# Layer normalization of a two-layer recurrent trunk: centering, root, folded parameters, and the order around the modulation chunks

## The reference

```python
mods = (silu(c) @ ada_w + ada_b).reshape(B, 3, 3, 1, D_MODEL)

def modulate(t, i):
    return t * (1.0 + mods[:, i, 1]) + mods[:, i, 0]

def residual(t, i, out, w):
    return _layer_norm(ALPHA * t + w * (1.0 + mods[:, i, 2]) * out, ln_g[i], ln_b[i])

x = residual(x, 0, _swiglu(modulate(x, 0), ...), 0.5)
# mixer: projection of modulate(x, 1), heads, output projection
x = residual(x, 1, mix, 1.0)
x = residual(x, 2, _swiglu(modulate(x, 2), ...), 0.5)
```

## Time and profile before

| | us |
|---|---|
| median of 3 runs | 2032.99 |
| lowest, highest | 2031.02, 2041.39 |
| the profiled execution's own time | 2035.65 |
| its span | 2033.8 |

### The profile page before, as it was taken

How to read it: one execution, slowest core, us unless ns; L and a number is a source line. 1 busy time by engine, 2 the same in 40 slices (tenths; PEclk the granted TensorE clock), 3 DMA queues, 4 the chain that set the end, 5 groups by cost and what they waited for, 6 DMA issues and landing times.

```text
span 2033.8 us, 33834 instructions
## 1 busy us (share of the span) xinstructions
PE 1812.7 (89%) x14564; PEld 1622.5 (80%) x14564; DVE 965.9 (47%) x1571; ACT 675.2 (33%) x927; POOL 223.5 (11%) x265
## 2 busy tenths in 40 slices
PE   6999998876899788999989999889759977799997
PEld 3899997775677567999979999788647756699996
DVE  2444445563333366454454444556443243665544
ACT  1332334352212235333353333444321122443333
POOL 1000012001000223000130001300010011410012
PEclk9999998888676678999999999998867665999999
DMA  8555545323232026444455554533322110434442
GB/s 302 187 206 188 176 149 190 98 89 130 94 95 68 18 76 212 144 147 153 148 176 197 179 200 148 177 132 104 109 73 95 49 36 32 142 114 154 148 146 78
DMA packets 85204, 272.37 MB, mean 134 GB/s; under 512 B 18976, under 2 KB 21312, under 8 KB 84800
## 3 DMA queue, kind: packets, MB, share of 16 engines
q1 hardware_dynamic: 85056, 270.22, 39.1%
HBM read 263.92 MB, written 6.26 MB: 133 GB/s over the span
## 4 chain that ended last, share of the span: by engine, by line
PE 77%; DVE 10%; ACT 5%; issue 3%; DMA 3%; POOL 2%; SPq 0%; DVEq 0%; ACTq 0%; POOLq 0%
PE psV L1767 10%; PE psV L1769 10%; PE psV L1768 10%; PE psA L1767 9%; PE psA L1768 8%; PE psA L1769 8%; DMA raw<-weights_dram 3%; PE psV L657 3%; PE psC L1782 2%; DVE wlo L2029 2%; PE psV L1793 2%; ACT whi L1928 1%; POOL ZT L2165 1%; PE psY L1782 1%; PE psA L1124 1%
## 5 line engine op out<-in xcount | busy, mean ns | idle before, releaser
L2029 DVE TENSOR_TENSOR wlo<-raw,whi 128x1024 fp32r<-128x1024 f32 x344 | 425.8, 1242 | 495.8 <-ACT whi L1928 493.8
L1928 ACT ACTIVATE whi<-raw 128x1024 fp32r<-128x1024 f32 x344 | 362.4, 1056 | 364.8 <-PE psV L1769 346.2
L1767 PE MATMUL psA<-XH,whi 128*128 128x320 f32 x1200 | 387.1, 323 | 50.6 <-DVE wlo L2029 34.4
L1768 PE MATMUL psA<-XL,whi 128*128 128x320 f32 x1200 | 379.9, 317 | 0.0
L1769 PE MATMUL psA<-XH,wlo 128*128 128x320 f32 x1200 | 379.4, 316 | 0.0
L1767 PEld LDWEIGHTS psA<-XH,whi 128*128 128x128 f32 x1200 | 234.4, 195 | 67.6 <-issue 62.7
L1767 PE MATMUL psV<-XH,whi 128*128 128x320 f32 x848 | 268.7, 317 | 13.2 <-DVE wlo L2029 7.2
L1769 PE MATMUL psV<-XH,wlo 128*128 128x320 f32 x848 | 264.9, 312 | 0.0
L1768 PE MATMUL psV<-XL,whi 128*128 128x320 f32 x848 | 264.9, 312 | 0.0
L1768 PEld LDWEIGHTS psA<-XL,whi 128*128 128x128 f32 x1200 | 234.5, 195 | 0.3
L1769 PEld LDWEIGHTS psA<-XH,wlo 128*128 128x128 f32 x1200 | 233.8, 195 | 0.0
(11 more groups left out here) (359 smaller groups left out, 2040.7 us busy)
## 6 DMA issues: line engine op xcount, KB each, us to landing
raw<-weights_dram SPq DMA_DIRECT2D x488, 512.0 KB, 3.4
ZS<-st_rw_dram SPq DMA_DIRECT2D x2, 768.0 KB, 4.5
S<-st_gla_dram SPq DMA_DIRECT2D x2, 768.0 KB, 4.4
o_glas_dram<-S SPq DMA_DIRECT2D x2, 768.0 KB
o_rws_dram<-ZS SPq DMA_DIRECT2D x2, 768.0 KB
CON<-consts_dram SPq DMA_DIRECT2D x1, 1288.5 KB, 10.2
XT<-xT_dram SPq DMA_DIRECT2D x1, 1280.0 KB, 9.8
yT_dram<-XT SPq DMA_DIRECT2D x8, 160.0 KB
```

The lines of the kernel that those rows point to most:

```text
L1767: mm(out, whi[:, n % SPL, k], hi[:, kt], start=first, stop=False)
L1768: mm(out, whi[:, n % SPL, k], lo[:, kt], start=False, stop=False)
L1928: activation(whi[:, n % SPL], raw[:, DENSE[n] % RAW], ACT.Copy).then_inc(hi_done, 1)
L2029: tt(wlo[:, n % SPL], raw[:, DENSE[n] % RAW], whi[:, n % SPL].bitcast(F32), ALU.subtract).then_inc(lo_done, 1)
```

## The change

- PLAN: "norm" comes directly after the product's step, ahead of all ada chunks.
- TensorE's `norm` opens both banks and multiplies ZSUM and QSUM before it waits for the last z and the last square.
- Centering: GpSimd's `center` is gone. VectorE subtracts the mean from ZT, tiles 0 and 1 ahead of the wait for the root, tile t + 2 behind the product of tile t.
- Root: ScalarE loads the table for Sqrt and takes the root; VectorE takes the reciprocal. ScalarE then loads the table for Silu where an FFN comes next.
- ln_g and ln_b of the norm before are folded into scale and shift of the modulation (in `unfold`), so that XM comes from ZT; XT is made by ScalarE one tile behind XM.
- Split of the next product's third chunk: ScalarE's part moves ahead of the last square, VectorE's part into `modulate`, at t == 3.
- GpSimd's sample modulation reads ZT and waits for `zn_ready`.

```diff
     def product(step, s, groups):
         chunks, left = two_groups(groups)
-        return [step] + chunks[:2] + [("norm", L, s)] + chunks[2:], left
+        return [step, ("norm", L, s)] + chunks, left
...
                 def norm(s):
-
-                    bank = bV.open()
                     pe.wait_ge(sem("zsum_ready"), s + 1)
-                    mm(bank[:, 0:TOK], con("mean1024", P), ZSUM[:], start=True, stop=False)
+                    means = []
+                    for x in (ZSUM, QSUM):
+                        bank = bV.open()
+                        mm(bank[:, 0:TOK], con("mean1024", P), x[:], start=True, stop=False)
+                        bV.close()
+                        means.append(bank)
                     pe.wait_ge(sem("z_ready"), (s + 1) * DT)
...
+                    def result(t):
+                        A.do(activation(XT[:, t], ZT[:, t], ACT.Identity, scale=lcol("ln_g", after, t),
+                                        bias=lcol("ln_b", after, t)), sem("x_ready"))
+
                     for t in range(DT):
                         if after is not None:
                             act.wait_ge(sem("zn_ready"), after * DT + t + 1)
...
+                        A.do(activation(XM[:, t, 0:SEQ], (XT if after is None else ZT)[:, t, 0:SEQ], ACT.Identity,
+                                        scale=scol(s, 1, t), bias=scol(s, 0, t)), sem("xm_prompt"))
+                        if after is not None and t:
+                            result(t - 1)
...
                 def product(n0, kts, s):
                     for d in range(DT):
-                        split_to(n0 + ((d + 1) * kts - 1) // 8 + 2)
+                        split_to(n0 + ((d + 1) * kts - 1) // 8 + (2 if d < DT - 1 else 3))
                         act.wait_ge(sem("z_ready"), s * DT + d + 1)
                         A.do(activation(SQ[:, d], ZT[:, d], ACT.Square), sem("sq_ready"))
 
-                    split_to(n0 + DT * kts // 8 + 2)
-
                 def norm(s):
+                    nc.scalar.preload_act_table(ACT.Sqrt)
                     act.wait_ge(sem("var_ready"), s + 1)
-                    rsqrt(A, VR[:], sem("sd_ready"))
+                    A.do(activation(VR[:], VR[:], ACT.Sqrt), sem("sd_ready"))
+                    if s % 3 != 0 and s < 3 * DEPTH - 1:
+                        nc.scalar.preload_act_table(ACT.Silu)
                     modulate(s + 1 if s < 3 * DEPTH - 1 else None, s)
...
                     if g == 3:
...
+                        s = 3 * L + i
+                        if s:
...
+                            V.settle()
+                            V.do(tt(rest, scale, affine("ln_b"), ALU.mult))
+                            V.settle()
+                            V.do(tt(shift, shift, rest, ALU.add))
+                            V.do(tt(scale, scale, affine("ln_g"), ALU.mult))
...
-                def modulate(s, after):
+                def modulate(s, after, n_next=0):
                     for t in range(DT + 2):
                         if t < DT and after is not None:
-
-                            vec.wait_ge(sem("zc_ready"), after * DT + t + 1)
                             V.do(tt(ZT[:, t], ZT[:, t], VR[:], ALU.mult), sem("zn_ready"))
+                            if t < DT - 2:
+                                V.do(tt(ZT[:, t + 2], ZT[:, t + 2], MN[:], ALU.subtract))
+                                V.settle()
+                        if t == 3:
+                            split_to(n_next + 2)
...
                     V.do(ts(VR[:], VR[:], 0.0, LN_EPS / ALPHA ** 2, ALU.max, ALU.add), sem("var_ready"))
-                    split_to(n_next + 2)
+                    for t in range(2):
+                        V.do(tt(ZT[:, t], ZT[:, t], MN[:], ALU.subtract))
                     vec.wait_ge(sem("sd_ready"), s + 1)
-                    modulate(s + 1 if s < 3 * DEPTH - 1 else None, s)
+                    V.do(nc.vector.reciprocal(VR[:], VR[:]))
+                    V.settle()
+                    modulate(s + 1 if s < 3 * DEPTH - 1 else None, s, n_next)
```

More of the change, by code:

```diff
@@ L1937, in modulate @@
                             act.wait_ge(sem("zn_ready"), after * DT + t + 1)
[L1938 to L1943, removed]
+                        if s is None:
+                            result(t)
+                            continue
+                        A.do(activation(XM[:, t, 0:SEQ], (XT if after is None else ZT)[:, t, 0:SEQ], ACT.Identity,
+                                        scale=scol(s, 1, t), bias=scol(s, 0, t)), sem("xm_prompt"))
+                        if after is not None and t:
+                            result(t - 1)
+                    if s is not None and after is not None:
+                        result(DT - 1)
                 def product(n0, kts, s):
                     for d in range(DT):
-                        split_to(n0 + ((d + 1) * kts - 1) // 8 + 2)
+                        split_to(n0 + ((d + 1) * kts - 1) // 8 + (2 if d < DT - 1 else 3))
                         act.wait_ge(sem("z_ready"), s * DT + d + 1)
                         A.do(activation(SQ[:, d], ZT[:, d], ACT.Square), sem("sq_ready"))
-                    split_to(n0 + DT * kts // 8 + 2)
                 def norm(s):
+                    nc.scalar.preload_act_table(ACT.Sqrt)
                     act.wait_ge(sem("var_ready"), s + 1)
-                    rsqrt(A, VR[:], sem("sd_ready"))
+                    A.do(activation(VR[:], VR[:], ACT.Sqrt), sem("sd_ready"))
+                    if s % 3 != 0 and s < 3 * DEPTH - 1:
+                        nc.scalar.preload_act_table(ACT.Silu)
                     modulate(s + 1 if s < 3 * DEPTH - 1 else None, s)
@@ L2043, in unfold, with affine @@
                         V.settle()
-                        V.do(ts(mods[:, i * 24 + 8:i * 24 + 16], mods[:, i * 24 + 8:i * 24 + 16], 1.0, None, ALU.add))
+                        shift, scale, rest = [mods[:, i * 24 + 8 * j:i * 24 + 8 * j + 8] for j in range(3)]
+                        V.do(ts(scale, scale, 1.0, None, ALU.add))
+                        s = 3 * L + i
+                        if s:
+                            def affine(name):
+                                k = PARC[name] + (s - 1) % 3 * DT
+                                return PAR[:, (s - 1) // 3, k:k + DT].unsqueeze(2).to_broadcast([P, DT, 9])
+                            V.settle()
[3 more added lines that the diff above has]
+                            V.do(tt(scale, scale, affine("ln_g"), ALU.mult))
                         V.mark(sem("mods_ready"))
@@ L2066, in product @@
                 def product(n0, kts, s, states=None):
+                    if s:
+                        vec.wait_ge(sem("x_ready"), s * DT)
                     for d in range(DT):
@@ L2157, in sums @@
                     G.mark(sem("zsum_ready"))
[L2159 to L2165, removed]
                 def modulate(s):
@@ L2170, in modulate @@
                     pool.wait_ge(sem("mods_ready"), s + 1)
[L2171 to L2173 removed]
                     for t in range(DT):
                         if s:
[L2176 to L2177 removed]
+                            pool.wait_ge(sem("zn_ready"), (s - 1) * DT + t + 1)
+                        G.do(tt(s8(mtmp[:, t % 2]), s8((ZT if s else XT)[:, t, SEQ:TOK]), by_sample(scol(s, 1, t, 1, DB)), ALU.mult))
                         G.settle()
```

13 lines of the change are left out of this document (4 added, 9 removed).

## The result

The changed kernel takes 2084.28 us in the median (2082.5 to 2086.92) against 2035.69 for the kernel before beside it (2031.02 to 2041.39): a ratio of 1.0238, 95% interval 1.0207 to 1.027. The forecast was 2070.5, with 2060 to 2082 as its range. The direction and the mechanism of the gaps hold; 2084.28 lies outside the range. The difference to the kernel before is 48.6 us, where the sum had 37.5: 11 us were missing from it. The other 2.7 of the 13.8 us are the kernel before, which had 2032.99 on record and has 2035.69 here.

What follows compares the result with a forecast made beforehand. The prediction took TensorE to bound the kernel, its gaps set by modulation chunk loads. 37.0 - 1.2 + 1.2 + 0.1 - 0.1 + 0.5 = 37.5 us on 2032.99 gave 2070.5, range 2060 to 2082.

Steps and rivals of the forecast that it cites:

- What bounds the gap: Behind the first four normalizations, modulation chunk loads queue behind VectorE's third-chunk split; 10.37 us from its end to the projection.
- D2's wlo: VectorE's split of the next product's third chunk, at the first normalization: ends at 320.6 instead of 311.36, +9.24 us.
- Rival A: Modulation chunk loads don't follow the third chunk's split; the arithmetic chain sets the start: 2030 us, not slower; chance 0.10.
- Copy 0.9 us after z, square 0.48, clamp 2.83 us after z: Start of the normalization: earlier mean copy gains 1.7 us, square without GpSimd's subtractions gains 0.7; clamp ends at 311.49.
- Reciprocal: In the normalization's root: VectorE's reciprocal of 128x320 takes 2.153 us; the root part loses 0.8 us.
- First XL: VectorE's first split activation after the normalization: x_split comes at 318.4, 2.8 us earlier than before.
- Next product: First projection matmul behind the first normalization moves from 321.73 to 331.0; the four gaps together cost 37.0 us.
- N4: Fifth normalization, no modulation chunks behind it: the next group starts at 1780.6 against 1780.47, +0.1 us.
- What comes back, and the clock at the gaps: Two first groups no longer paced by split activations, -1.2 us; lower granted clock after four longer gaps, +1.2 us.
- Rival B: GpSimd's sample modulation holds up VectorE's loop at four normalizations: 12.8 us more, so 2083; chance 0.10.
- Folding: Folding ln_g and ln_b: five times three VectorE operations on 72 elements; 0 to 5 us, 0.5 taken.
- case C: The five-chunk burst in the gaps takes 9.5 us instead of 10.37: 2067; included in the forecast's 0.80 chance.

Runs made afterwards that it cites:

- e1: The changed kernel with VectorE's split of the next product's third chunk moved back ahead of the copy of the mean: 2038.31 us, ratio 1.0029.
- e2: The kernel before with only VectorE's split of the next product's third chunk moved to t == 3 of the modulation: 2064.61 us, ratio 1.0172.
- e3: The changed kernel with VectorE's split of the next product's third chunk at t == 6 instead of t == 3: 2103.14 us, a single execution.
- e10: The changed kernel with only the folding moved, from unfold to VectorE's product at its second output tile: 2070.06 us, ratio 1.0176.
- e7: e1 with the folding moved from unfold to VectorE's product at its second output tile: 2027.12 us, ratio 0.9969.
- e8: The kernel before with three more VectorE operations of 72 elements in unfold, whose results nobody reads: 2043.02 us, ratio 1.0047.
- e11: e7 with the norm behind the first two modulation chunks again, as in the kernel before: 2030.34 us, ratio 0.9993.
- e12: e7 with six of eight modulation chunks in the gap, one behind the next product's fourth step and one behind its seventh: 2033.13 us, ratio 1.0.
- e9: e7 with three of eight modulation chunks in the gap and five behind the next product's fourth step: 2077.51 us, ratio 1.02.

## Why the prediction was wrong

By its own steps:

- **What bounds the gap** (the stream of A chunks, with D2's wlo ahead of it): right. (The rows of N0 to N3 repeat to 0.5 us, 11.47 to 11.94 from wlo's start to the next product, and not to 0.1 as the prediction has it; the sum doesn't rest on that.) e1 and e2 show it from both sides, e3 with a dose. Rival A falls.
- **Copy 0.9 us after z, square 0.48, clamp 2.83 us after z:** measured 0.89, 0.49, 2.80. **Reciprocal** 2.153 forecast, 2.145 measured.
- **First XL** 9.7 us after z forecast, 9.53 measured; **D2's wlo** 11.94 forecast, 11.60 measured. The 0.3 us were won by the end of the reciprocal, which began 0.1 us ahead of the second subtraction's end; the loop itself took what was forecast.
- **Next product** 22.3 us after z forecast; 22.25, 21.9, 21.8 and 23.5 measured. **N4** 12.0 forecast, 11.9 measured.
- **What comes back, and the clock at the gaps:** -1.2 and +1.2 forecast. With them the gaps were to make 37.1 us and made 38.2 and 36.7.
- **Rival B:** GpSimd's operations hardly hold VectorE up; the products took 491 ns in the median and 589 at most, the subtractions 485 and 589. The exclusive lock that the Trainium skill describes ("SBUF — State Buffer", "SBUF: two separate sides") shows beside centering in the kernel before but at 0.1 us an operation here. The rival had the right mechanism and the wrong place: it shows at the folding, below.
- **Folding: the step that failed.** The term was "0 to 5 us if all were on the path; I take 0.5". The first mixer got 14.4 and 12.9 us longer in the profiles. By the medians, each taken against the kernel before beside it, the operations' place costs 11.5 us (changed against e10: 48.6 and 37.1), 12 (e1 against e7: 6.2 more and 5.9 less) and 10 (e8). Two things were wrong. I counted the operations by their own length and took a low point of the bounds, although those in the first mixer stand on a chain: the kernel before's own rows for the place show VectorE going from the scale's addition to the mixer's next operation in 0.87 us, and the operations made it 2.39, since the first took 1.07 beside GpSimd's. (Those in the second mixer cost nothing.) And I bounded the effect by that length. A mixer whose clock is at the lower level for 165 of 267 us has a second price for a delay. The prediction weighed the clock at the gaps only.

With the term at 11.5 us the sum would have been 48.5, with the 14.4 of the first profile 51.4, against 48.6 measured. That the rest of the sum came out so close is in part luck: the gaps made 35.4 to 38.2 us in the three profiles with the split at t == 3 in the changed kernel, and the second mixer of one kernel differs by some us between executions.

Not settled: why 1.5 us in the first mixer bring the lower clock for 25 to 50 us more. That it doesn't happen in the second mixer fits with the delay not arising there; whether it would with a delay of 1.5 us wasn't tried. Of the profiles without the operations seven have 263 to 267 us there (before twice, e2, e7, e10, e11, e12), and all five with them have 277 to 282 (changed twice, e1, e3, e8). But e9's 274.0, without them, says that they aren't the only way into it, and three of e8's ten times that they don't always lead there.

## What to carry to other kernels

A step that is cheap and off the chain may be the release of a ring buffer: before moving it, ask which load in the DMA queue waits for it and what is queued behind that load. Here a split of 1.2 us, moved by 9 us, delayed five transfers and with them the next product by the same 9 us, four times, while the arithmetic that the change was about did become 3 us quicker each time. Small operations added to a chain between engines are priced by the chain and by what runs beside them (here 1.07 us for one that takes 0.23 elsewhere), and where TensorE is granted its lower clock for much of the stretch, by what they do to the clock too.

## What the runs showed of the hardware that I had not expected

- With a delay of 1.5 us in it, a stretch of 263 to 267 us with a mean granted clock of 0.67 to 0.70 (seven profiles) took 277 to 282 us with 0.62 to 0.64 (five profiles); the matmuls are the same ones. One profile without the delay had 274.0 us with 0.64.
- VectorE's operation with two inputs of 128x72 took 1.07 us where GpSimd's operation of 128x384 (0.99 us) started with it, and 0.23 us elsewhere.
- The time from issue of the first of five 512 KB loads until all five are used was 10.0 to 10.7 us in 15 of 16 gaps of the changed kernel, e10, e2 and e3, where SP had stood for 12.3 us or more ahead of it, 9.9 to 10.5 in the second profile of the changed kernel, and 10.2 to 10.7 in the kernel before, where it had stood for 3.3 to 4.4. A longer rest doesn't make the burst quicker (case C of the prediction didn't come).
- The same kernel's executions differ by more than its gaps can explain: the kernel before lay between 2013.95 and 2043.07 us, and in the profiles of all kernels here the second mixer, in which the changes cost nothing, took 249.0 to 263.1 us.
